# One streaming encoder layer on one core: the opening's first three tiles run ahead, and nine other steps are placed elsewhere

## What is computed

```
xn = RMSNorm(x)
z  = xn @ w_in        # q | k | v | forget logits | pooling input u | memory query | 3 gates
A  = forgetting attention(q, k, v, cumsum(log_sigmoid(forget logits + b_f)))   # 8 heads x 64
B  = (trailing means of u over 2/4/8/16 tokens - u) @ w_pool * s_pool          # 4 groups x 128
C  = attention of the memory query into 256 memory tokens                       # 4 heads x 128
h  = x + (sum_b sigmoid(gate_b) * (branch_b @ w_b)) @ w_out
x  = h + relu(RMSNorm(h) @ w_up)^2 @ w_down
y  = RMSNorm(x)
```

## Time and profile before

| | |
|---|---|
| median of 3 runs | 1940.26 us (1939.59 to 1940.54) |
| the profiled execution | 1939.99 us |
| its span, first to last instruction | 1938.3 us |
| PE busy | 1900.1 us (98%) |
| DVE, ACT, POOL busy | 1223.0, 843.7, 516.3 us |
| DMA | 104 GB/s in the mean |

### The profile page before, as it was taken

The page is one execution under the profiler, slowest core; times in us unless marked ns, Lnnn a source line. Parts: engine busy times, 40 slices in busy tenths (PEclk is TensorE's granted clock), DMA queues, the critical chain, the costliest instruction groups (busy, mean ns, idle before and its releaser), DMA issues. The chain is left out here.

```text
span 1938.3 us, 32954 instructions
## 1 busy us (share of the span) xinstructions
PE 1900.1 (98%) x12587; PEld 1865.1 (96%) x12587; DVE 1223.0 (63%) x2285; ACT 843.7 (44%) x1671; POOL 516.3 (27%) x547
## 2 busy tenths in 40 slices
PE   7999999999999999999999999999999999999998
PEld 7999999999999999999999999999999999999997
DVE  6675545454557665554333467687787877777765
ACT  6444435353546543442223332344444544444445
POOL 1003324150612122000000003276554333333320
PEclk9999999999999999999999999999999999999999
DMA  6451311312266633453232322233433433333323
GB/s 188 121 133 50 93 47 49 99 35 86 62 228 203 205 114 101 151 165 110 84 89 84 93 83 76 85 107 88 124 88 88 124 88 88 91 89 88 88 93 98
DMA packets 243601, 202.40 MB, mean 104 GB/s; under 512 B 16750, under 2 KB 217966, under 8 KB 243317
## 3 DMA queue, kind: packets, MB, share of 16 engines
q1 hardware_dynamic: 243445, 200.29, 34.2%
HBM read 166.62 MB, written 33.64 MB: 103 GB/s over the span
## 5 line engine op out<-in xcount | busy, mean ns | idle before, releaser
L1616 PE MATMUL ps<-act_hi,w_hi 128*128 128x384 f32 x1128 | 386.7, 343 | 1.2 <-DVE fox_q_lo L2646 0.9
L1616 PE MATMUL ps<-act_hi,w_lo 128*128 128x384 f32 x1128 | 377.9, 335 | 0.0
L1616 PE MATMUL ps<-act_lo,w_hi 128*128 128x384 f32 x1128 | 377.5, 335 | 0.0
L581 DVE TENSOR_TENSOR w_lo<-w_raw,w_hi 128x512 fp32r<-128x512 f32 (+1 forms) x200 | 197.6, 988 | 124.1 <-ACT w_hi L563 123.3
L1600 PE MATMUL ps<-ffs_hi,w_hi 128*128 128x288 f32 x832 | 245.6, 295 | 2.2 <-DVE h L2579 2.2
L1600 PE MATMUL ps<-ffs_hi,w_lo 128*128 128x288 f32 x832 | 245.3, 295 | 0.0
L1600 PE MATMUL ps<-ffs_lo,w_hi 128*128 128x288 f32 x832 | 244.9, 294 | 0.0
L1585 PE MATMUL ps<-bp_hi,pw_hi 128*128 128x288 f32 x784 | 231.5, 295 | 0.2 <-DVE pw_lo L2534 0.2
L1585 PE MATMUL ps<-bp_lo,pw_hi 128*128 128x288 f32 x784 | 231.3, 295 | 0.0
L1585 PE MATMUL ps<-bp_hi,pw_lo 128*128 128x288 f32 x784 | 231.2, 295 | 0.0
L563 ACT ACTIVATE w_hi<-w_raw 128x512 fp32r<-128x512 f32 (+1 forms) x200 | 152.7, 763 | 161.1 <-PE ps L1600 119.3
(11 more groups left out here) (352 smaller groups left out, 4181.4 us busy)
## 6 DMA issues: line engine op xcount, KB each, us to landing
w_raw<-in_w_down_dram SPq DMA_DIRECT2D x112, 256.0 KB, 3.2
pair_raw<-in_w_up_dram SPq DMA_DIRECT2D x28, 1024.0 KB, 5.4
w_raw<-in_w_in_dram SPq DMA_DIRECT2D x44, 512.0 KB, 4.2
merged<-prod SPq DMA_DIRECT2D x48, 192.0 KB, 2.0
prev<-merged SPq DMA_DIRECT2D x48, 192.0 KB, 4.1
foxs_vraw<-in_cache_fox_v_dram SPq DMA_DIRECT2D x8, 1024.0 KB, 6.1
foxs_kraw<-in_cache_fox_k_dram SPq DMA_DIRECT2D x7, 1024.0 KB, 5.4
x_in<-in_x_prompt_dram SPq DMA_DIRECT2D x8, 512.0 KB, 4.5
```

The lines of the kernel that those rows point to most:

```text
L581: nc.vector.tensor_tensor(W[c % 2][1][:, 0:kt, :], w_raw[c % 2][:, 0:kt, :], W[c % 2][0][:, 0:kt, :].bitcast(F32), ALU.subtract).then_inc( ...
L1616: last = nc.tensor.matmul(bank(b)[:, 0:width], W[k][a][:, t, :], moving[z][:, t, j * width:(j + 1) * width], start=(t == 0 and n == 0), st ...
```

## The change

The opening: tile 2 gets its own pair of banks (4 and 5), so that its transposes wait for no low part; ACT and DVE do the parts of the first three tiles ahead of the rest; and `EARLY` starts products after the third tile's transposes in place of the sixth's. The load of `b_f` is issued ahead of tile 4 in place of after the weights.

Elsewhere: pooling group 3 moves from half 0 to half 1 of the first q block; ACT gets a one-element exponential behind the high part of group 3; the last step of the samples is cut in two for both branches, `turned_out` and what follows it one half later (and the values of k = 0 one half later too), while PE's wait for the last sample's result stands at piece 2 of the first `br` block in place of pieces 0 to 2; the reciprocal of a memory step is done ahead of the next queries' low part; the first keys' low part is done ahead of four memsets; and at two places of the last stage `down_add` is done ahead of the splits.

```diff
-        put(("u", g + 1, 0, 0) if g + 1 < BT else ("q", 0, 0, 0), "pool", g)
+        put(("u", g + 1, 0, 0) if g + 1 < BT else ("q", 0, 0, 1), "pool", g)
...
-        put(where[3 + s], "sample", 0, s)
+        put(where[3 + s + s // (3 * NB)], "sample", 0, s)
     put(where[28], "mem_parts", 0)
+    put(where[29], "sample", 0, 3 * NB + 1)
...
+    put(where[7 + BT * QT + 5 + 3 * NB], "sample", 1, 3 * NB + 1)
...
+        def next_queries(s):
+            return s % QT == 2 and s // QT + 1 < MH
...
         def norm_banks(t):
+            k = 4 if t == 2 else 2 * (t % 2)
+            return ps[:, k:k + 2, :].rearrange("p a (b c) -> p (a b) c", c=P)
...
+            sp.dma_start(f_b[:], b_f.rearrange("l h -> h l"), allow_slow_non_contiguous=True).then_inc(fs["b_in"], 16)
             load_tile(4)
...
-            EARLY = {5: (0,), 6: (1,), 7: (2,), 8: (3, 4, 5), 9: (6, 7), 10: (8, 9, 10, 11)}
+            EARLY = {2: (0,), 3: (1,), 4: (2,), 5: (3,), 6: (4, 5), 7: (6,), 8: (7,), 9: (8, 9), 10: (10, 11)}
...
-                if t >= 2:
+                if t >= 3:
                     pe.wait_ge(xn["done"], t - 1)
...
-                            if s.i == 1:
+                            if s.i == 1 and j == 2:
                                 pe.wait_ge(sa["o_done"], NB)
...
+            stats(0)
+            stats(1)
+            stats(2)
+            turned_hi(0)
+            stats(3)
+            turned_hi(1)
+            forget_hi(act)
+            turned_hi(2)
+            split_hi(act, 1)
+            stats(4)
...
+                if g == BT - 1:
+                    nc.scalar.activation(small[:, 18:19], eps_t[:], ACT.Exp)
...
+            scaled(0)
+            scaled(1)
+            scaled(2)
+            turned_lo(0)
+            turned_lo(1)
+            forget_lo(dve)
+            turned_lo(2)
+            scaled(3)
+            split_lo(dve, 1)
+            scaled(4)
...
-                if 1 <= s <= M_UNITS:
+                if 1 <= s <= M_UNITS and not next_queries(s - 1):
                     reciprocal(u - 1)
...
+                early = kind == "down" and i == 0 and s in (0, SEAM // 2 - 2)
+                if early:
+                    down_add(s, i)
```

More of the change, by code:

```diff
@@ L653, in norm_banks @@
         def norm_banks(t):
-            return ps[:, 2 * (t % 2):2 * (t % 2) + 2, :].rearrange("p a (b c) -> p (a b) c", c=P)
+            k = 4 if t == 2 else 2 * (t % 2)
+            return ps[:, k:k + 2, :].rearrange("p a (b c) -> p (a b) c", c=P)
         def fin_banks(t):
@@ L743, in _ @@
             load_weights(sp, 3)
-            sp.dma_start(f_b[:], b_f.rearrange("l h -> h l"), allow_slow_non_contiguous=True).then_inc(fs["b_in"], 16)
             sp.dma_start(s_col[:], s_pool.rearrange("l (g p) -> p (l g)", p=P),
@@ L1430, in sample @@
                         values()
-                    if i == NB:
-                        turned_out()
+                elif part == 1 and i == NB:
+                    turned_out()
                 elif part == 1:
@@ L1728, in _ @@
             nc.scalar.activation(col(RC, 3), eps_t[:], ACT.Sqrt)
-            for t in range(NT + MT + 2):
+            stats(0)
[8 more added lines that the diff above has]
+            stats(4)
+            for t in range(5, NT + MT + 2):
                 if t < NT + MT:
                     stats(t)
[L1732 to L1739, removed]
+                turned_hi(t - 2)
+                if t in (6, 8, 9, 11):
+                    early(plan[(6, 8, 9, 11).index(t)])
+            early(plan[4])
             split_hi(act, 2)
-            early(plan[4])
             early(plan[5])
@@ L1825, in mem @@
                     exponent(u, ps[:, s % 2, 0:NMEM], mp[s % 3][:], M_SCALE)
-                if s % QT == 2 and s // QT + 1 < MH:
+                if next_queries(s):
                     queries_hi(s // QT + 1)
@@ L1878, in sample @@
                     nc.scalar.activation(p, p, ACT.Copy, scale=col(RC, c)[rows]).then_inc(sa["p_ready"], 1)
-                elif part == 0:
+                elif part == 1 and i == NB:
                     out_low()
@@ L2188, in _ @@
             nc.vector.memset(u_t[0][:], 0.0).then_inc(po["clear"], 1)
-            for t in range(NT + MT + 2):
+            scaled(0)
[8 more added lines that the diff above has]
+            scaled(4)
+            for t in range(5, NT + MT + 2):
                 if t < NT + MT:
                     scaled(t)
[L2192 to L2197, removed]
+                turned_lo(t - 2)
             split_lo(dve, 2)
@@ L2367, in mem @@
                                           ps[:, 4, 0:2 * P]).then_inc(at_s["o_done"], 1)
-                if s % QT == 2 and s // QT + 1 < MH:
+                if next_queries(s):
+                    reciprocal(u)
                     queries_lo(s // QT + 1)
@@ L2395, in first @@
                     dve.wait_ge(at_s["pv_over"], PAIRS + M_PAIRS * k)
+                    keys_lo(a, 0, 0)
                     for n in range(2):
@@ L2404, in first @@
                     last.then_inc(sa["q_clear"], 1)
-                keys_lo(a, 0, part)
-                if part == 1:
+                else:
+                    keys_lo(a, 0, 1)
                     dve.wait_ge(sa["q_clear"], k + 1)
@@ L2467, in sample @@
                     masked_out()
-                if part == 0 and i == NB:
+                if part == 1 and i == NB:
                     out_sum()
@@ L2751, in _ @@
                 if kind == "down":
-                    down_add(s, i)
+                    if not early:
+                        down_add(s, i)
                     if s == CHUNKS - 2 and i >= KT // 2:
```

## The result

| | before | after |
|---|---|---|
| median of 9 runs | 1940.54 us (1939.59 to 1941.44) | 1944.86 us (1942.44 to 1946.71) |
| the profiled execution | 1939.99 | 1943.18 |
| its span | 1938.3 | 1941.5 |

The ratio is 1.0021, with a 95% interval of 1.0012 to 1.0029: slower by 4.3 us. The forecast was 1937.4, its range 1933.5 to 1941.0. The runs also lie wider apart than before, 4.3 us against 1.9.

A forecast was written before the change was run, and what follows sets the result against it. PE, busy 98% of the span, was taken as the bound, so only its idle stretches and clock could move the time. Gains and losses at each place summed to -2.6 us: 1939.99 to 1937.4, range 1933.5 to 1941.

The forecast's parts named there:

- The q block: First q block: moved pooling group and table load make fox_q_hi 3.1 us later, PE waits some 5 us: +3.1 us.
- rival 2: At the k block the clock falls in the 5 us wait, costing 1 to 3.4 us: say 1939.5; chance 0.25.
- Rival 3: Clock falls at the k block and stays low 13.6 us, costing 6.8: 1944.2 us, slower than before; chance 0.07.
- Rival 4: First q block not late because the k split finds an earlier slot, 3.1 becomes -0.6: 1933.7 us; chance 0.05.
- The opening: Kernel start: first product at 16.9, key block at 48.4 against 49.70, second key block's wait shrinks: -1.6 us.
- `down_add`: Two places of the last stage: waits removed by doing it ahead of the splits, -0.9 and -0.4 us.
- the table load off the first exponential: At the first exponential: the load leaves, so PE's waits behind it shrink: -0.7 us (0 to -1.3).
- the end of the samples: Start of memory attention: removed waits outweighed by late mem_k_hi and mqs_lo, PE waits 2.5 at first scores: +1.3 us.
- the reciprocals: Memory steps: two more waits for mem_p, the first goes (-0.9), the second shrinks (-1.2): together -2.1 us.
- the last sample of k = 1: Wait of 0.8, 0.9 with refill, hidden by the half of 2.1 us put between: -0.9 us.
- the first keys: Wait of 0.6 us at the first keys, half taken back by the queries' copies behind the memsets: -0.4 us.
- Rival 1: Handover at the samples' end not late, queries land sooner and DVE catches up, 1.3 becomes -2.9: 1933.2 us; chance 0.2.

The follow-up runs named there:

- fill kernel: The changed kernel with 36 more matmuls, whose results nobody reads, on PE in front of the k block, where PE waits: 1942.11 us median.
- the version with two edits more: Changed kernel, pooling group 3 back, exponential before ACT's wait, forget sum behind second key block's low weights, k = 0 values at old half, last transposes before memory parts: 1934.09 us.
- `down_add` alone: The kernel before the change with only down_add ahead of the splits at the two places of the last stage: 1940.42 us in its one profiled run.

## Why the prediction was wrong

**The q block** (+3.1; measured +7.4) is the step that failed. Its own text: "ACT reaches it behind the copy of 116.24, so it runs 116.6 to 117.7". ACT reached it then, but the weights had not landed. I asked what stands in front of the split on its engine and not when its input arrives, although the sum moved the step from 125.31 to 116.6. That made 2.1 us on ACT and DVE: `fox_q_hi` came at 131.56 in place of 129.4, `fox_q_lo` at 133.55 in place of 131.4. The load put in front of the store took them away again (wait 5.20, 2.3 at PE's rows). Another 1.7 are rival 2, the clock, to which I gave 0.25 as a case of its own. The fill kernel shows it. That is 4.0 of the 4.3 by which the step was off; the other 0.3 no run assigns. The rule of the Trainium skill that I had weighed against the sum ("TensorE: Matmul & The Clock Gate", "HAM oscillation — how this bites in real kernels") was right here and my own reading, that one idle stretch at the end proves little, was not. The price that the rival gave it, 1 to 3.4, held. Rival 3 fell: the clock rose again after 11 to 18 products. Rival 4 fell too: the k split found no earlier slot, it started at 118.65.

**The opening** (-1.6; measured -0.46 in the profile, -0.3 in medians). The mechanism was right up to the first product. That the key block came at 47.48, before the foreseen 48.4, was the clock of this one execution. Two terms were mis-sized. I gave 0.3 for late weights at the key blocks and let the wait before the second shrink; the waits are 1.10 and 0.25. And the clock was entered as one lag, while it differs from run to run by up to 8 products at half pace.

**`down_add`** (-0.9 and -0.4; measured 0.0 and -0.2). The -0.2 is no effect that shows: in the eleven profiles of kernels with this edit the second step lies between -0.66 and +0.36, and in two without it at -0.13 and -0.03. Its waits went, but behind each stands weights' work on the same DVE or a DMA, and PE only met that instead. I had seen this for the second place (a high half that waits for its DMA) and not for the first.

**Right, with their mechanism**: the table load off the first exponential (-0.77 for -0.7); the end of the samples, with `mem_k_hi` held by the transfer of the queries and 2.25 of wait for `mqs_lo` (foreseen 2.5), +1.10 for +1.3; the reciprocals (-2.18 for -2.1), with 0.34 left of the wait after the second (foreseen 0.4); the last sample of k = 1 (-0.96 for -0.9); the first keys (-0.26 for -0.4). Rival 1 fell with the second of these.

**The median.** The forecast was made against one profile. The profile after says +3.2, the medians +4.3. The opening explains little of the difference: the profiles of before and after both stood 0.3 to 0.4 better there than the mean of their kind. In the fill kernel the median moved by 1.0 more than PE's rows did, so a likely reason is that the profiled execution had a cheap case of the clock at the k block. The profile without the exponential, with 18 slow products, shows that dearer ones exist; of this kernel none was caught, so this is inferred.

## What to carry to other kernels

When a step is moved forward on an engine, look up when each of its inputs lands, not only what stood before it: a load that took 11.6 us was invisible as long as its user came late. Price a new wait of PE of some us with the slow products behind it, above all if the range is to hold. And when a wait is removed, ask which instruction of the engine that ended it comes next: that is often the weight split, and nothing is gained.

## What the runs showed of the hardware that was not expected

The clock fell in waits of 7.49, 5.90, 5.87 and 5.20 us, and of 2.46 us at the k block, but not in the waits of 1.9 to 2.7 us before the first memory scores in six profiles, nor in one of 0.96. What differs between a wait of 2.46 with a fall and one of 2.68 without was not tried. In the opening the clock was already up when the wait of 2.46 us ended in five of the ten profiles with the new order, and fell again behind it; in the other five it rose only after the wait, between 2.8 and 6.2 us behind the first product. One of the five that fell, the version with two edits more (first product, then the granted clock behind it):

```profile
16.76 0.41 PE L1229 MATMUL ps<-act_hi,w_hi 128*128 128x384 f32 x1 [2.46 <-DVE act_lo L2199]
```
```profile
17.00:20.00 3.00, 3.00 (x13) 2.90 (x13) 2.96 (x4) 1.97 (x6) 0.00 (x0) 0.55 0.30 79
```

One wait of that length is not needed for it. With the old opening the clock also rose near 17.5 and fell near 21 in two of four profiles, and no wait of PE there is longer than 1.59 us. `down_add` alone is one of them:

```profile
21.21 1.94 PE L1234 MATMUL ps<-ident,xs 128*128 128x128 f32 x8 [1.59 <-DVE act_lo L2185]
```
```profile
20.00:23.00 3.00, 1.79 (x9) 1.82 (x10) 2.96 (x4) 2.97 (x6) 0.00 (x0) 0.61 0.62 210
```

The Trainium skill, "TensorE: Matmul & The Clock Gate", section "Part 1: The HAM clock gate", says that the number of slow products of one kernel differs between runs with the phase of the gate at kernel start. The counts here, 5 to 13, differ as it says; that the phase is the cause no run here shows.

A load of 512 KB issued behind a store of 2112 KB took 11.7 us to land, and 5.2 in front of it.
